# Products with the low halves of the weights last in each tile, and GpSimd's low halves in four pieces

## What is computed

```
mod = silu(c) @ W_ada + b_ada            # shift/scale/gate, two sets
h   = RMSNorm(x) * (1 + scale_m) + shift_m
[q | k | v | p] = h @ W_in               # 4096 columns
A:  causal pooling of p (windows 2/4/8/16), per-group linear, scale, projection
B:  differential attention of q, k, v, 8 heads, per-head RMSNorm, projection
x  += gate_m * ((sig(g_A) * y_A + sig(g_B) * y_B) @ W_out)
h2  = RMSNorm(x) * (1 + scale_f) + shift_f
x  += gate_f * PEER(h2)                  # 8 heads, product keys 2 x 128, top 16 of 16384 experts
out = RMSNorm(x)
```

## Time and profile before

| | |
|---|---|
| median of 3 runs | 1854.78 us (1854.44 to 1858.8) |
| the profiled execution | 1861.06 us, span 1859.1 us |
| TensorE busy | 1585.6 us (85%), 7052 products |
| VectorE busy | 1327.0 us (71%) |
| ScalarE busy | 547.7 us (29%) |
| GpSimd busy | 622.5 us (33%), of it low weights 11 x 4647 ns |
| products of `mm3` | 640 each of L491, L492, L493, mean 369, 353 and 352 ns |
| low weights on VectorE (L1135) | 42 x 2290 ns |
| granted TensorE clock, mean | 0.937 |

### The profile page before, as it was taken

The page is one execution under the profiler, slowest core; times in us unless marked ns, Lnnn a source line. Parts: engine busy times, 40 slices in busy tenths (PEclk is TensorE's granted clock), DMA queues, the critical chain, the costliest instruction groups (busy, mean ns, idle before and its releaser), DMA issues.

```text
span 1859.1 us, 20730 instructions
## 1 busy us (share of the span) xinstructions
PE 1585.6 (85%) x7052; PEld 1171.7 (63%) x7052; DVE 1327.0 (71%) x2591; ACT 547.7 (29%) x1337; POOL 622.5 (33%) x527
## 2 busy tenths in 40 slices
PE   3998999998997979999979999999999989998000
PEld 1786877776876979888868888884444434443000
DVE  5766456667556698898985888886566566667998
ACT  2433234444623632111115888880000000000001
POOL 1000000000002512534563555556444444445773
PEclk7999999999998989999989999999999999999555
DMA  8423311123421436999987989899999999999995
GB/s 315 156 111 138 136 68 49 66 91 151 178 91 66 180 135 222 350 326 321 369 307 283 323 310 317 318 319 369 409 409 409 411 410 409 409 409 409 370 379 218
DMA packets 124232, 498.19 MB, mean 268 GB/s; under 512 B 13920, under 2 KB 14176, under 8 KB 113760
## 3 DMA queue, kind: packets, MB, share of 16 engines
q0 software_dynamic: 73728, 268.47, 38.2%
q1 hardware_dynamic: 50400, 228.41, 32.9%
HBM read 492.11 MB, written 4.72 MB: 267 GB/s over the span
## 4 chain that ended last, share of the span: by engine, by line
PE 31%; DVE 29%; DMA 25%; ACT 5%; issue 4%; DVEq 3%; ACTq 1%; POOL 1%; SPq 0%; POOLq 0%
DMA ring<-in_up,idx 17%; PE bank L754 9%; DVE accum L1671 8%; DMA ring<-in_down,idx 7%; PE bank L491 6%; PE bank L492 6%; PE bank L493 5%; DVE ring L1454 4%; PE bank L741 2%; DVE acc_ada L1116 1%; DMA raw<-in_ada 1%; POOL ring L1696 1%; ACT h2T L1035 1%; DVE wlo L1135 1%; ACT h2T L1040 1%
## 5 line engine op out<-in xcount | busy, mean ns | idle before, releaser
L754 PE MATMUL bank<-h2T,stream 128*128 128x256 f32 x2048 | 453.5, 381 | 11.4 <-ACTq L1069 11.4
L767 PE MATMUL bank<-stream,wmat 128*128 128x512 f32 x1024 | 443.3, 596 | 12.4 <-DMA stream<-in_up 8.3
L1696 POOL DMA_INDIRECT ring<-in_down,idx x256 | 314.5, 1229 | 377.2 <-DVE pre L1454 293.7
L1671 DVE SCALAR_TENSOR_TENSOR accum<-ring,share,accum 128x1024 f32<-128x1024 f32 x256 | 328.8, 1284 | 139.1 <-DMA ring<-in_up,idx 128.7
L754 PEld LDWEIGHTS bank<-h2T,stream 128*128 128x128 f32 x2048 | 386.7, 191 | 62.5 <-issue 11.7
L1454 DVE CUSTOM_DVE_ANT_0 ring<-ring,h2row 128x1024 f32<-128x1024 f32 x256 | 307.0, 1220 | 73.7 <-DMA ring<-in_down,idx 69.8
L767 PEld LDWEIGHTS bank<-stream,wmat 128*128 128x128 f32 x1024 | 195.6, 191 | 259.5 <-issue 246.0
L1696 POOL DMA_INDIRECT ring<-in_up,idx x256 | 256.6, 1002 | 219.6 <-DVE accum L1671 181.3
L491 PE MATMUL bank<-hT_hi,whi 128*128 128x512 f32 (+1 forms) x640 | 236.4, 369 | 29.6 <-DVE hT_lo L1169 12.3
L1705 POOL TENSOR_TENSOR wlo<-raw,whi 128x2048 fp32r<-128x2048 f32 x11 | 51.1, 4647 | 610.7 <-ACT whi L789 610.7
L492 PE MATMUL bank<-hT_lo,whi 128*128 128x512 f32 (+1 forms) x640 | 225.8, 353 | 0.0
(11 more groups left out here) (211 smaller groups left out, 1647.7 us busy)
## 6 DMA issues: line engine op xcount, KB each, us to landing
stream<-in_downT SPq DMA_DIRECT2D x128, 512.0 KB
stream<-in_up SPq DMA_DIRECT2D x128, 512.0 KB
raw<-in_ada SPq DMA_DIRECT2D x24, 1024.0 KB, 5.4
raw<-in_w_query SPq DMA_DIRECT2D x16, 1024.0 KB, 4.8
raw<-in_w_xp SPq DMA_DIRECT2D x4, 1024.0 KB, 6.4
raw<-in_w_gateA SPq DMA_DIRECT2D x4, 1024.0 KB, 4.8
raw<-in_w_branchP SPq DMA_DIRECT2D x4, 1024.0 KB, 4.8
raw<-in_w_q SPq DMA_DIRECT2D x4, 1024.0 KB, 4.8
```

Source lines behind the costliest of these rows:

```text
L754: last = pe.matmul(bank[:, 4 + i % 2, 0:DT], stream[:, i % RING, k * P:(k + 1) * P], h2T[:, k, GB * P:S], start=(k == 0), stop=(k == KT - 1))
L767: last = pe.matmul(bank[:, 2 * tb + half, :], wmat[:, i, tb * P:(tb + 1) * P], stream[:, (ET + i) % RING, half * S:(half + 1) * S], start= ...
L1671: dve.scalar_tensor_tensor(accum[:, b, :], ring[slot][:, :], share[:, b, k:k + 1], accum[:, b, :], ALU.mult, ALU.add).then_inc(sum_done, 1)
L1696: pool.indirect_dma_start(out=ring[slot][:, :], out_offset=None, in_=table, in_offset=bass.IndirectOffsetOnAxis(ap=idx[:, b, k:k + 1], axi ...
```

## The change

In every stage but pool and v the eight slices of a tile first go through the two products with the high weights, and then once more through the product with the low weights. The wait for `lo_ready` stands ahead of this second loop, in the first tile of a chunk. In pool and v nothing changes. GpSimd makes the low weights of its eleven chunks in four instructions of 512 columns, and signals after the last.

```
-                pe.wait_ge(lo_ready, n + 1)
+                if stage in ("pool", "v"):
+                    pe.wait_ge(lo_ready, n + 1)
...
-                            last = mm3(bank[:, BANK[t], 0:toks.stop - toks.start], wh[:, k, m * P:(m + 1) * P],
-                                       wl[:, k, m * P:(m + 1) * P], ah[:, k, toks], al[:, k, toks],
-                                       k == 0, k == KT - 1)
+                            dst = bank[:, BANK[t], 0:toks.stop - toks.start]
+                            pe.matmul(dst, wh[:, k, m * P:(m + 1) * P], ah[:, k, toks], start=(k == 0), stop=False)
+                            pe.matmul(dst, wh[:, k, m * P:(m + 1) * P], al[:, k, toks], start=False, stop=False)
+                        if m == 0:
+                            pe.wait_ge(lo_ready, n + 1)
+                        for k in range(KT):
+                            last = pe.matmul(dst, wl[:, k, m * P:(m + 1) * P], ah[:, k, toks], start=False,
+                                             stop=(k == KT - 1))
                         last.then_inc(tile_ready, 1)
...
-                pool.tensor_tensor(wlo[:, n % 2].rearrange("p a b -> p (a b)"),
-                                   raw_w(n).rearrange("p a b -> p (a b)"),
-                                   whi[:, n % 2].bitcast(f32).rearrange("p a b -> p (a b)"), ALU.subtract)\
-                    .then_inc(lo_ready, 1)
+                for k in range(0, KT, 2):
+                    last = pool.tensor_tensor(wlo[:, n % 2, k:k + 2].rearrange("p a b -> p (a b)"),
+                                              raw_w(n)[:, k:k + 2].rearrange("p a b -> p (a b)"),
+                                              whi[:, n % 2, k:k + 2].bitcast(f32).rearrange("p a b -> p (a b)"),
+                                              ALU.subtract)
+                last.then_inc(lo_ready, 1)
                 pool.drain()
                 pool.sem_inc(qraw_free, 1)
```

## The result

| | before | after |
|---|---|---|
| median | 1854.88 us (1854.44 to 1859.4, 7 runs) | 1864.81 us (1861.45 to 1867.93, 7 runs) |
| the profiled execution | 1861.06 us, span 1859.1 us | 1864.71 us, span 1862.9 us |
| granted TensorE clock, mean | 0.937 | 0.935 |

After against before is a ratio of 1.0035, with a 95% interval of 1.0021 to 1.0049: the change costs 6.5 us (3.9 to 9.1). That is just past the 0.3% that can be told from no change. The forecast was +3.0; what came is the price that the first rival gave, +6.5.

A forecast was written before the change was run, and what follows sets the result against it. TensorE bounds the kernel until about 620 us, VectorE's routing from there. Terms 3.2 + 2.7 + 0.3 - 3.2 = +3.0 us on the profiled 1861.06 give 1864.1, for the median 1857.8; range 1851.5 to 1862.5.

The forecast's parts named there:

- the first rival: Near 619 us GpSimd's next piece gets in after each VectorE operation; sum +6.5 us, 1861.3, slower; chance 0.18.
- The first tile of xp: First xp projection tile: low-weight products pile up after the last k and the clock rises later; +3.2 us, bounds 1.2 to 4.2.
- The clock's term: First xp tile: 4.3 us of products at the low clock behind the last wait add 2.0 us.
- The woven chunks: q, k and gateB chunks: TensorE reaches odd attention steps early and waits longer, at 255.09, 457.49, 480.89; +2.7 us, bounds 0 to 4.5.
- Four pieces at the start: GpSimd's low weights near 42.36 us: pieces help VectorE little, three more instruction starts cost; +0.3 us, bounds -1.9 to +1.0.
- The meeting near 620: VectorE's eight low parts wait for only GpSimd's first piece, ending at 623.9 instead of 627.1; -3.2 us, bounds -3.2 to +0.3.
- VectorE keeps going: Near 620 us, after GpSimd's first piece, VectorE runs all its eight low parts before GpSimd's next piece; basis of -3.2 us.
- A second step: GpSimd's later pieces near 620 are hidden, other chunks' pieces meet no critical VectorE work, removed query waits give nothing: 0 us.
- TensorE's waits in the queries: Query chunks: some 10.8 us of visible waits for low weights lie almost wholly behind VectorE's routing; removing them gives nothing.
- The cover: TensorE's 11.4 us stop at the expert tiles, caused by VectorE's routing, hides the query waits; without it up to 10.8 us would show.

The follow-up runs named there:

- the order alone: New order of products as in the change, GpSimd's low weights in one instruction as before, against the kernel before: ratio 1.0057, +10.6 us.
- without the first tile: New order with whole GpSimd instructions, but the first tile of the first xp chunk in the old order, against the kernel before: 1.004, +7.4 us.
- ahead of the queries: New order in all chunks before queryA, old order in the queries, one GpSimd instruction, against the kernel before: 1.0043, +8.0 us.

## Why the prediction was right and wrong

**The time**, 1857.8 forecast, range 1851.5 to 1862.5: the ratio puts the change at +6.5, on 1854.78 that is 1861.3, inside the range but over the 0.3% to the slower side, which I gave 0.25. The two medians themselves lie 9.9 apart, a little beyond the ratio's interval (9.1), and the median after, 1864.81, lies past the range. It came by the first rival's mechanism, the two engines in turn, and at its price, but that the price fits is luck. In the traces the terms are 2.2 + 3.7 + 0.1 + 0.8 = +6.8, against the rival's 3.2 + 2.7 + 0.3 + 0.3, and the last of them contains a second meeting that the rival did not have.

**The first tile of xp** (3.2 us: order 1.2, clock 2.0): 2.2 measured. The direction of both held. The clock's term was mis-sized: I charged the low clock for 4.3 us of unbroken products behind the last wait, a length read from other places. The clock rose 1.2 us after the last k's first product (54.15), ahead of the end of the tile, so it cost 0.55. The order cost 1.5.

**The woven chunks** (2.7 us, three stalls of 0.9): the first stretch of the table grew by 5.9, less 2.2 for the first tile, so 3.7 in these traces; the run without them saved 3.0. Of the three stalls I had named, 255 grew by 0.94 as priced, 480 by 1.77, and 457 did not: it shrank from 0.73 to 0.29, and the wait at 448.62 before, 450.09 after, grew by 0.95 in its place. 308 stayed, as forecast. What I had put at nothing is the steps that wait less now, by some 2 us together with the small new waits set against them, and the clock behind the longer waits. A fall to half speed for 3.4 us is worth 1.7 us; two followed the stalls, and a fall that before had at 532 us is missing after. So of the 3.7 about 1.7 is clock and 2.0 the stalls. That the missing fall comes from the change is not shown: two kernels with the old order up to the queries (the ones with four and with eight pieces and the new order in the queries) lack it too. Without it the woven chunks cost 5.3.

**Four pieces at the start** (+0.3): from the start of the eight-column operation to the end of the two behind it VectorE needed 3.58 us before (42.36 to 45.94) and 3.70 after (40.54 to 44.24): +0.1. Right. Three more starts cost 0.43 us by GpSimd's own rows (5.03 against 4.60 to 4.62 undisturbed), inside the bound of 0.9.

**The meeting near 620** (-3.2): this step failed, and it turned the answer. +0.8 came. "VectorE keeps going" was read out of one row, GpSimd at 594.33 in 5.11 us. There at most two low parts were left when GpSimd asked, too few to tell "after all eight" from "after the next". All runs with pieces say that the engines take turns: the wait is cut into as many parts as there are pieces, and all are paid. But they do not take turns every time. These are two low parts of VectorE each, the first of each pair under way when GpSimd asks, in the kernel before (GpSimd at 594.33) and in the order alone (at 632.56):

```profile
594.12 0.87 DVE L1169 SCALAR_TENSOR_TENSOR hT_lo<-h2T,modc,hT_hi 128x256 fp32r<-128x256 f32 x2
```

```profile
632.30 5.22 DVE L1186 SCALAR_TENSOR_TENSOR hT_lo<-h2T,modc,hT_hi 128x256 fp32r<-128x256 f32 x2
```

The second low part was let through at 594, as in all thirteen traces, and held up at 632. I can't show from these runs why.

**A second step failed with it**: that GpSimd's later pieces and the shorter query chunks change nothing on the path. By the new order TensorE frees the slots 0.87 us sooner, and GpSimd's next low weights then fall on the last low parts. With whole instructions this costs 4.35 us (11.65 against 7.30), with four pieces 0.8 to 1.0. So in this change the pieces make good most of a damage that the order itself does.

**TensorE's waits in the queries** (nothing, covered by VectorE's routing): right, 88.00 against 88.02 us from MAX8 to the gathers. The wait at 678 was to become two microseconds shorter, because VectorE was to be 3.2 us earlier; VectorE came later, and it grew by 1.5. The cover's limit showed when VectorE's routing was made 5.9 us earlier: then the old order loses 3.05 us and the new one 0.43.

## What to carry to other kernels

When two engines share a port, ask for every instruction that the change makes earlier whom it will now meet, on either engine; a wait that is removed behind a cover still moves what it released. Cutting the long instruction of such a pair in pieces doesn't free the other engine where they take turns, as here near 620, but it bounds what a second meeting can cost. Cheaper than either is to set off the critical one first: one call moved by a few lines on a third engine gave 3.5 us alone and 6.1 with the order restricted to where it helps.

## What the runs showed of the hardware

- VectorE and GpSimd, both with their inputs in SBUF, went in turn after every instruction near 620 us, where both had one ready: eight against eight took 6.86 and 6.87 us from 616.85 and 616.56, where alone they take 3.25 and 5.60. Near 594 GpSimd's instruction took 5.11 us instead of 4.62 and let a second low part of VectorE go first, so the turn is not taken every time.
- The granted clock fell to 1.2 GHz shortly behind waits of TensorE of 2.15 and 1.93 us, in all four runs that had them (the change, the order alone, without the first tile, ahead of the queries), and in none of the nine others, where they were at most 1.52 and 0.16. Three of these four then lacked the fall near 532 us that before had, but so did two of the nine, so these runs don't show whether a fall is moved or added.
- In the first tile, with two products in every 1.32 us, the clock rose from 1.2 to 2.4 GHz 10.0 to 11.4 us after the first product in the four runs with the new order there; with three products in the same interval it rose after 3.0 to 6.1 us in all the others.
